# Sublayer boundaries, chunk sums and level differences put in another order in a two-layer hybrid decoder trunk

## What is computed

```python
for l in range(DEPTH):                       # DEPTH = 2
    mod = (silu(c) @ w_ada[l] + b_ada[l]).reshape(bsz, 3, 3, 1024)
    x = sublayer(x, ffn1)                    # swiglu: (silu(a) * b) @ w_out, width 2816
    x = sublayer(x, token_mixing)            # HGRN2, stick-breaking, dilated attention; gates; @ w_out
    x = sublayer(x, ffn2)
# sublayer: h = rms_norm(x, g_pre) * (1 + scale) + shift
#           x = x + res_w * gate * rms_norm(fn(h), g_post)
```

## Time and profile before

| what | value |
|---|---|
| median of 3 runs | 3118.58 us (3118.45 to 3123.26) |
| the profiled execution's own time | 3121.1 us |
| its span | 3119.3 us |
| PE busy | 2929.9 us (94%) |
| DVE busy | 1541.3 us (49%) |
| ACT busy | 1005.0 us (32%) |
| POOL busy | 193.1 us (6%) |
| SP's DMA queue | 32.4% of 16 engines |
| chain that ended last | PE 85%, DVE 7%, ACT 3%, issue 2% |
| granted TensorE clock, mean | 0.975 of full |

### The profile page before, as it was taken

How to read it: one execution, slowest core, us unless ns; L and a number is a source line. 1 busy time by engine, 2 the same in 40 slices (tenths; PEclk the granted TensorE clock), 3 DMA queues, 4 the chain that set the end, 5 groups by cost and what they waited for, 6 DMA issues and landing times.

```text
span 3119.3 us, 40607 instructions
## 1 busy us (share of the span) xinstructions
PE 2929.9 (94%) x16999; PEld 2558.1 (82%) x16999; DVE 1541.3 (49%) x2236; ACT 1005.0 (32%) x1455; POOL 193.1 (6%) x188
## 2 busy tenths in 40 slices
PE   6999898989999988999989989899899999899998
PEld 5888897777788788889988879877777887888897
DVE  5555236777344446542255552477753554453323
ACT  3322124444422323222242221354443232332212
...
GB/s 238 176 189 189 109 96 61 61 62 68 41 55 82 81 127 104 189 135 95 97 88 195 186 167 89 88 62 75 51 52 41 68 95 81 109 122 95 102 89 55
DMA packets 358854, 324.53 MB, mean 104 GB/s; under 512 B 12300, under 2 KB 305552, under 8 KB 357776
## 3 DMA queue, kind: packets, MB, share of 16 engines
q1 hardware_dynamic: 357136, 319.77, 32.4%
...
HBM read 313.43 MB, written 6.29 MB: 102 GB/s over the span
## 4 chain that ended last, share of the span: by engine, by line
PE 85%; DVE 7%; ACT 3%; issue 2%; POOL 0%; ACTq 0%; DVEq 0%; POOLq 0%
PE PS L769 25%; PE PS L771 24%; PE PS L770 24%; PE PS L973 2%; PE PS L786 2%; DVE WL L1573 1%; PE PS L1048 1%; PE PS L1010 1%; PE PS L1070 1%; PE PS L1034 1%; PE PS L1025 1%; PE PS L1022 1%; PE PS L832 1%; ACT WH L1164 1%; PE PS L779 1%
## 5 line engine op out<-in xcount | busy, mean ns | idle before, releaser
L769 PE MATMUL PS<-HH,WH 128*128 128x512 f32 (+1 forms) x2512 | 974.3, 388 | 27.3 <-DVE WL L1562 10.3
L771 PE MATMUL PS<-HH,WL 128*128 128x512 f32 (+1 forms) x2512 | 948.7, 378 | 0.0
L770 PE MATMUL PS<-HL,WH 128*128 128x512 f32 (+1 forms) x2512 | 946.9, 377 | 0.0
L1562 DVE TENSOR_TENSOR WL<-RAW,WH 128x2048 fp32r<-128x2048 f32 x142 | 325.5, 2292 | 515.5 <-ACT WH L1164 515.5
L769 PEld LDWEIGHTS PS<-HH,WH 128*128 128x128 f32 x2512 | 475.7, 189 | 116.7 <-DVE WL L1573 13.7
L771 PEld LDWEIGHTS PS<-HH,WL 128*128 128x128 f32 x2512 | 475.0, 189 | 88.7
L770 PEld LDWEIGHTS PS<-HL,WH 128*128 128x128 f32 x2512 | 476.1, 190 | 82.0 <-issue 2.9
L1164 ACT ACTIVATE WH<-RAW 128x2048 fp32r<-128x2048 f32 x142 | 271.8, 1914 | 792.6 <-PE PS L771 792.6
L769 PE MATMUL PS<-GH,WH 128*128 128x256 f32 x1408 | 405.0, 288 | 18.2 <-DVE WL L1562 17.5
L771 PE MATMUL PS<-GH,WL 128*128 128x256 f32 x1408 | 403.7, 287 | 0.0
L770 PE MATMUL PS<-GL,WH 128*128 128x256 f32 x1408 | 403.3, 286 | 0.0
...
## 6 DMA issues: line engine op xcount, KB each, us to landing
...
RAW<-in_w_in SPq DMA_DIRECT2D x132, 512.0 KB, 4.7
...
AWB<-in_w_ada SPq DMA_DIRECT2D x5, 2048.0 KB, 16.0
...
```

What stands on the lines that cost most here:

```text
L769: pe.matmul(o, ah, bh, start=start, stop=skip, skip_group_check=skip)
L770: pe.matmul(o, ah, bl, start=False, stop=skip, skip_group_check=skip)
L771: return pe.matmul(o, al, bh, start=False, stop=stop or skip, skip_group_check=skip)
L1562: dve.tensor_tensor(wl[:, 0:n], RAW[g % 2][:, 0:n], wh[:, 0:n].bitcast(F32), ALU.subtract).then_inc(w_low, 1)
```

## The change

- **Weight halves.** `from_stage` counts groups from the end e of a rows stage. Group e-2 is split into the second buffers (WXH, WXL) and e-1 into the slot of e-3's predecessor, both free once group e-4 is used; e goes to the slot of e-3, e+1 to the other second buffers.
- **Rows product.** The first row group goes by four columns at a time, (second half, j 4 to 7) first, each with its own wait for its banks; after `merge` these are waits for single products of br_mul.
- **Modulation.** In FFN 1 the last chunk's sum, its copy and its two column operations stand at mixing item 3, step 0, and the sums alternate banks 4 and 5.
- **Boundary.** A DVE addition halves each squared piece of x (`square_pair`, 128x256, 48 in all: 8 for each of five boundaries and 8 at the start), and `x_sum` is one matmul. The orders of squares, roots and pair additions on ACT and DVE move, and the second half's `x_sum` on PE goes one step earlier.
- **Mixing.** `a_diff` moves from POOL to DVE, one level ahead. The preparation stands behind the takes and its third step is cut in two (k = 3 and 4). Turning a tile moves from step 1 to 2 on PE and from 2 to 3 on DVE. Tiles 4 to 7 get banks of their own. The first branch group's low half stands in the last item at step 3.

The diff, without context, blank lines, the two hunks that only renumber `ada_cols`, and part of the indentation:

```diff
@@ -437,16 +437,15 @@
-def beside(g):
-    return g % NG in (G_MIX, G_MIX + 1, G_FFN2, G_FFN2 + 1) or (g % NG < 2 and now[0] + g // NG > 0)
+def from_stage(g):
+    g += NG * (now[0] > 0)
+    return min((g - e - n * NG for n in range(3) for e in ROW_ENDS if g - e - n * NG >= -2), default=99)
-    if beside(g):
-        back = max((e for e in ROW_ENDS if e <= g), default=0) - 3
-    else:
-        back = g - (4 if beside(g - 2) else 2)
+    d = from_stage(g)
+    back = g - {-1: 3, 0: 3, 1: 4, 2: 3, 3: 3}.get(d, 2)
@@ -456,7 +455,11 @@
-    return (WXH[g % 2], WXL[g % 2]) if beside(g) else (WH[g % 2], WL[g % 2])
+    d = from_stage(g)
+    if d in (-2, 1):
+        return WXH[d > 0], WXL[d > 0]
+    slot = (g + (d in (-1, 0))) % 2
+    return WH[slot], WL[slot]
@@ -475,7 +478,10 @@
-    return tile if tile < 4 else tile % 2
+    return tile if tile < 8 else tile % 2
+def ada_bank(f, i):
+    return 2 if (f, i) == (0, FI // 2 - 1) else 4 + i % 2
@@ -712,7 +718,8 @@
-            sp.wait_ge(ada_out, at(ada_out, ADA_CHUNKS[0]))
+            sp.wait_ge(ada_part, at(ada_part, KT * (ADA_CHUNKS[0] + 1)))
+            sp.wait_ge(ada_out, at(ada_out, ADA_CHUNKS[0] - 1))
@@ -781,10 +788,8 @@
-        pe.wait_ge(x_sq, at(x_sq, 8 * p + 4 * half + q + 1))
-        for e in range(2):
-            mm = pe.matmul(y_at(half, 0), ones, XSQ[q][:, e, :],
-                           start=(q == 0 and e == 0), stop=True, skip_group_check=True)
+        pe.wait_ge(x_pair, at(x_pair, 8 * p + 4 * half + q + 1))
+        mm = pe.matmul(y_at(half, 0), ones, XSQ[q][:, 0, :], start=(q == 0), stop=True, skip_group_check=True)
@@ -809,8 +814,10 @@
-                if not half and p and (u, i) == (1, 1) and k >= KT // 2:
-                    x_sum(p, 1, k - KT // 2)
+                if not half and p and (u, i) == (1, 1) and 3 <= k <= 5:
+                    x_sum(p, 1, k - 3)
+                    if k == 5:
+                        x_sum(p, 1, 3)
@@ -824,15 +831,6 @@
-        def ada(i):
-            pe.wait_ge(ada_part, at(ada_part, i * KT + (ADA_BEFORE[f] + 2) * KT))
-            pe.wait_ge(ada_out, at(ada_out, ADA_BEFORE[f] + i))
-            for q in range(4):
-                mm = pe.matmul(PS[:, 4, q:q + 1], AACC[i % 2][:, q * P:(q + 1) * P], ones[:, 0:1],
-                               start=True, stop=True)
-            mm.then_inc(ada_sum, 1)
@@ -840,16 +838,22 @@
-                    ada(i - 1)
-        if n == FI // 2:
-            ada(FI // 2 - 1)
-    def rows_product(g0, n, rh, rl, ready, b, bank_free=None):
+                    ada(f, i - 1)
+    def ada(f, i):
+        pe.wait_ge(ada_part, at(ada_part, i * KT + (ADA_BEFORE[f] + 2) * KT))
+        pe.wait_ge(ada_out, at(ada_out, max(ADA_BEFORE[f] + i - 1, 0)))
+        for q in range(4):
+            mm = pe.matmul(PS[:, ada_bank(f, i), q:q + 1], AACC[i % 2][:, q * P:(q + 1) * P], ones[:, 0:1],
+                           start=True, stop=True)
+        mm.then_inc(ada_sum, 1)
+    def rows_product(g0, n, rh, rl, ready, b, bank_free):
-            wh = WH[(g0 + i) % 2][:, :].rearrange("p (k c) -> p k c", k=2)
-            wl = WL[(g0 + i) % 2][:, :].rearrange("p (k c) -> p k c", k=2)
+            wh, wl = (w[:, :].rearrange("p (k c) -> p k c", k=2) for w in halves_of(g0 + i))
@@ -859,9 +863,9 @@
-            for half in (1, 0) if i == 0 else (0, 1):
-                for j in range(KT):
-                    if i == 0 and bank_free:
+            for half, j0 in ((1, 4), (0, 0), (0, 4), (1, 0)) if i == 0 else ((0, 0), (0, 4), (1, 0), (1, 4)):
+                for j in range(j0, j0 + 4):
+                    if i == 0 and j == j0:
@@ -899,8 +903,10 @@
+            if (half, j) == (1, 4):
+                pe.wait_ge(x_done, at(x_done, 8 * b))
-                pe.wait_ge(ada_out, at(ada_out, ADA_BEFORE[f] + chunks(l, f)))
+                pe.wait_ge(ada_out, at(ada_out, ADA_BEFORE[f] + chunks(l, f) - (chunks(l, f) == FI // 2)))
@@ -934,7 +940,7 @@
-        if k0 == 0:
+        if k0 == 0 and tile >= 8:
@@ -1084,7 +1090,7 @@
-        if k == 1 and m and TILE0[m] - 1 in TURN_OF:
+        if k == 2 and TILE0[m] - 1 in TURN_OF:
@@ -1127,9 +1133,10 @@
+    def merged_free(half, j):
+        pe.wait_ge(br_mul, at(br_mul, {(1, 4): KT - 2, (0, 0): KT - 1}.get((half, j), KT)))
-        if i == 0:
-            pe.wait_ge(br_mul, at(br_mul, KT))
@@ -1143,10 +1150,13 @@
+                if (m, k) == (3, 0):
+                    pe.wait_ge(*taken(2))
+                    ada(0, ADA_CHUNKS[0] - 1)
-        rows_product(G_WO, 4, lambda k: HH[:, k, :], lambda k: HL[:, k, :], merged, 3 * l + 1)
+        rows_product(G_WO, 4, lambda k: HH[:, k, :], lambda k: HL[:, k, :], merged, 3 * l + 1, merged_free)
@@ -1239,14 +1249,16 @@
-            if q in (1, 2) and not last:
-                square_x(b + 1, 0, 2 * q - 2)
-                square_x(b + 1, 0, 2 * q - 1)
-        root_y(b, 1)
+            if q < 2 and not last:
+                square_x(b + 1, 0, 2 * q)
+                square_x(b + 1, 0, 2 * q + 1)
+            root_y(b, 1)
+            if j == 1:
+                root_y(b, 1)
@@ -1497,6 +1509,11 @@
+    def square_pair(p, half, q):
+        dve.wait_ge(x_sq, at(x_sq, 8 * p + 4 * half + q + 1))
+        dve.tensor_tensor(XSQ[q][:, 0, :], XSQ[q][:, 0, :], XSQ[q][:, 1, :], ALU.add).then_inc(x_pair, 1)
@@ -1538,14 +1555,25 @@
-            if q:
-                pair_add(b, 1, q - 1)
+            if q and not last:
+                square_pair(b + 1, 0, q - 1)
+            if q in (1, 3):
+                pair_add(b, 1, q // 2)
+        if not last:
+            square_pair(b + 1, 0, 3)
+        pair_add(b, 1, 2)
-        inputs(b + 1, 0, lambda q: residual(b, 1, q))
+        def second(q):
+            residual(b, 1, q)
+            if q:
+                square_pair(b + 1, 1, q - 1)
+        inputs(b + 1, 0, second)
+        square_pair(b + 1, 1, 3)
@@ -1585,10 +1613,10 @@
+                if (i, u) == (FI // 2 - 1, 1) and n == FI // 2:
+                    ada_columns(f, i - 1)
-        for i in range(min(n, FI // 2 - 2), n):
-            ada_columns(f, i)
@@ -1617,7 +1645,7 @@
-        dve.tensor_copy(MOD[:, 4 * ch:4 * ch + 4], PS[:, 4, 0:4]).then_inc(ada_out, 1)
+        dve.tensor_copy(MOD[:, 4 * ch:4 * ch + 4], PS[:, ada_bank(f, i), 0:4]).then_inc(ada_out, 1)
@@ -1696,6 +1724,7 @@
+        if k == 4:
@@ -1713,6 +1742,16 @@
+    def a_diff(h, k):
+        n = A_LEVELS * h + k
+        dve.wait_ge(p_log, at(p_log, 3 * h + 3))
+        dve.wait_ge(v_decay, at(v_decay, max(n - 1, 0)))
+        w = P >> k
+        b = level_view(AB[h % 2][:, :], k)
+        dve.tensor_tensor(level_view(AD[n % 2][:, :], k), b,
+                           b[:, :, w // 2 - 1:w // 2].broadcast_to([P, SEQ // w, w]), ALU.subtract).then_inc(v_diff, 1)
@@ -1726,6 +1765,10 @@
+        if k == 0:
+            a_diff(h, 0)
+        if k + 1 < A_LEVELS:
+            a_diff(h, k + 1)
@@ -1869,14 +1912,14 @@
-        if (m, k) in PREPARE_AT:
-            a_prepare(*PREPARE_AT[(m, k)])
-        if k == 2 and m and TILE0[m] - 1 in TURN_OF:
+        if (m, k) in PREPARE_AT:
+            a_prepare(*PREPARE_AT[(m, k)])
+        if k == 3 and TILE0[m] - 1 in TURN_OF:
@@ -1907,6 +1950,9 @@
+        for q in range(4):
+            square_pair(0, half, q)
+    for half in range(2):
@@ -1915,18 +1961,24 @@
-        dve.wait_ge(ada_out, at(ada_out, ADA_CHUNKS[0]))
-        columns(l, 4 * ADA_FIRST, 4 * (ADA_ALL - ADA_OWN), 2, (1, 2), (0, 1))
-        dve.wait_ge(ada_cols, at(ada_cols, 7))
+        dve.wait_ge(ada_out, at(ada_out, ADA_CHUNKS[0] - 1))
+        columns(l, 4 * ADA_FIRST, 4 * (ADA_ALL - ADA_OWN - 1), 2, (1,), (0, 1))
+        dve.wait_ge(ada_cols, at(ada_cols, 6))
+                if (m, k) == (3, 0):
+                    ada_columns(0, ADA_CHUNKS[0] - 1)
+                    dve.wait_ge(ada_out, at(ada_out, ADA_CHUNKS[0]))
+                    columns(l, 4 * (ADA_ALL - ADA_OWN - 1), 4 * (ADA_ALL - ADA_OWN), 6, (2,), ())
+                    dve.wait_ge(ada_cols, at(ada_cols, 8))
+                if (m, k) == (NM - 1, 3):
+                    low(G_BR)
-        low(G_BR)
@@ -1958,25 +2010,12 @@
-    def a_diff(h, k):
-        n = A_LEVELS * h + k
-        pool.wait_ge(p_log, at(p_log, 3 * h + 3))
-        pool.wait_ge(v_decay, at(v_decay, max(n - 1, 0)))
-        w = P >> k
-        b = level_view(AB[h % 2][:, :], k)
-        pool.tensor_tensor(level_view(AD[n % 2][:, :], k), b,
-                           b[:, :, w // 2 - 1:w // 2].broadcast_to([P, SEQ // w, w]), ALU.subtract).then_inc(v_diff, 1)
-        if k < A_LEVELS:
-            a_diff(h, k)
```

More of the change, by code:

```diff
@@ L1948, in _ @@
                     dve.wait_ge(ada_out, at(ada_out, ADA_BEFORE[1] + chunks(l, 1)))
[L1949 to L1950 removed]
+                    columns(l, 4 * (ADA_ALL - ADA_OWN), 72, 8, (), (2,))
+                    dve.wait_ge(ada_cols, at(ada_cols, 10))
                     if l + 1 < DEPTH:
[L1952 to L1953 removed]
+                        columns(l + 1, 0, 4 * ADA_FIRST, 10, (0,), ())
```

(1 more changed line is left out.)

8 lines of the change are left out of this document (2 added, 6 removed).

## The result

| | before | changed |
|---|---|---|
| median | 3120.92 us (3118.45 to 3125.54) | 2991.52 us (2987.59 to 2996.35) |
| again, in a later run of both | 3120.02 us | 2988.49 us (2987.42 to 2989.18) |
| the profiled execution's own time | 3121.1 us | 2996.35 us |
| span | 3119.3 us | 2994.6 us |

The ratio is 0.9584, with a 95% interval of 0.9564 to 0.9605. The forecast was 2992 us.

What follows compares the result with a forecast made beforehand. PE, busy 94% of the span, bounds the kernel by its work, granted clock and idle time. Seven terms sum to 126.8 us, 3121.1 to 2994.3; the median stood 2.5 lower, so 2992 us was forecast, range 2974 to 3024.

Steps and rivals of the forecast that it cites:

- Joint phase: Ahead of six joint phases: 4.39 us waits for a group's low half go, 26.3 us, plus 13.2 of low clock: 39.5 us.
- Boundary: Pair sums to second half, five boundaries: 32.0 us for 39.3, less 0.4 for clock, 6.9 each: 34.5 us.
- the boundary stays a DVE chain: Rival: eight more additions between residuals and inputs, so each boundary gains 2 us, not 6.9: 3017 us; chance 0.10.
- The 0.4 us taken off for clock: In each boundary: average deduction for a low-clock stretch that may follow the new waits, 7.3 us gain becoming 6.9.
- Chunk sum: Modulation sum at the first FFN in: two waits, 15.2 us, go, with 1.8 of sums and 4.0 of clock: 21 us.
- Merge and into w_out: Merge: two waits shortened by 2.4 us each plus 5.4 of clock, 10.2; wait in front of w_out goes, 6.6 us.
- Mixing: Mixing heads: four heads gain 10 us, the other eight 5, less 2: 13 us, bounds -12 and +25.
- The 2 us taken off for bank and second turned cv item: In mixing: 1 us off in each layer for a tile's bank margin and DVE's softplus ahead of the second turned item.
- First inputs: At the start: eight square sums, 4.2 us, go, but eight DVE additions precede the first scaled input: 2 us, 0 to 4.
- The rival in which new waits pull it down: Rival: five boundaries and four heads each lose 2.5 us to one more low-clock stretch: 3014 us; chance 0.07.
- The shared port: DVE in mixing: POOL's differences stretch its instructions; moving them returns 40 us against 51 added, with QL's mean at 0.42.

Runs made afterwards that it cites:

- u_sums: The changed kernel with its new boundary orders, but two matmuls for each sum of squares and no halving additions on DVE: 3000.83 us.
- u_bound: The changed kernel with the old boundary: old orders on ACT, DVE and PE, two matmuls per sum of squares, no halving additions: 3035.86 us.
- i_order: The changed kernel with DVE scaling inputs 0 to 4 and forming low parts 0 to 3 ahead of the second half's first residual in five boundaries: 2976.03 us.
- u_chunk: The changed kernel with the last chunk's sum, its copy and two column operations back at the end of the first FFN in: 3016.14 us.
- u_merge: The changed kernel with the first branch group's low half back behind the last item and w_out's first row group waiting for the last branch product: 3003.58 us.
- a_again: The changed kernel itself, unaltered, measured again beside the others on the same chip to show its spread: 2988.49 us.
- u_pool: The changed kernel with the level differences back on POOL at their old place, all else kept: 3005.23 us.

## Why the prediction was right, and where its reasons were not

The forecast was 2992 us, the medians are 2991.52 and 2988.49, and term by term:

- **Joint phase, term 39.5:** as argued, wait and clock together; undoing it costs 38.9 by the trace and 44 in the medians.
- **Boundary, term 34.5:** measured 33.5. The waits of the order followed stood nearly as forecast: 0.2 at the first sum, 0.93 for YSQ, 2.0 for HL one column later, 1.9 at the third and fourth sums (1.47 measured), 0.6 at the fourth column (0.32), none ahead of the second half. But one reason failed: the text counted the eight matmuls saved in each boundary (0.52 us each, half of the 8.3) as work taken off PE's path. u_sums has them back and is no later at full clock. The gain is that of the orders, by u_bound, and i_order shows that DVE's chain is still the bound; that the moved orders gain by shortening this chain is argued, as they were undone all at once. The 0.4 us taken off for clock was 0.3: of the three low stretches in the first profile two cost nothing and one, behind PE's last wait (at 1539.8), 1.5 us. What the rival "the boundary stays a DVE chain" said of the mechanism was true; its price of 2 us was not.
- **Chunk sum, term 21:** 21.3 to 22.3 by the trace of u_chunk.
- **Merge and into w_out, terms 10.2 and 6.6:** 17.5 in the profiled execution of u_merge, 14 in the median. Merge's residual wait is 0.83, forecast 0.8.
- **Mixing, term 13:** 14.4 less 4.7 for merge's wait, plus 1.8 for the sums moved in, 11.5; by a_again's profile, whose mixings have less low clock, 17.6. The term lies between the two. Head 0 waits 2.21, 0.67 and 0.90 us for a forecast 2.5, 0.8 and 1.2. The 2 us taken off for bank and second turned cv item were wrong: PE has no wait there. That the term came out is in part luck: it named AS as the largest gain at hand, but AS and QL together fell by 0.8 us only, and the 5.2 us of VT, which it did not price, went whole. It also treated takes and differences as separate gains; each without the other keeps half of the waiting saved or less.
- **First inputs, term 2:** 1.7 between the two profiles, but undoing the halving at the start costs less than 1 us (u_sums reaches the first FFN out 262.1 us after the first sum, the changed kernel's two profiles 262.3 and 261.3). The clock differs there: the low level at the start ends at 65.3 us before, at 62.1 in u_sums, at 72.1 and 69.6 in the changed kernel. So what the halving alone is worth here stays open.
- **The clock:** 54.2 us of PE's work left the low level, 25 us at 0.46; the terms name 22.6 (13.2, 4.0 and 5.4) and hold part of the 4.7 behind AV. The rival in which new waits pull it down was partly there: three of five boundaries have a stretch of 3.4 us (at 1140.4, 1539.8 and 2604.7), the others none; a_again has one in four of five. The rival's price of 2.5 us each was too high: they cost 1.5 or nothing. The Trainium skill ("TensorE: Matmul & The Clock Gate", "HAM oscillation") tells of a kernel whose waits of some 3 to 5 us for a DMA between groups of matmuls lower the clock each time; in these traces a wait of 2.0 us with 0.93 before it does so in some boundaries and not in others.
- **The shared port.** QL's mean went to 0.415 us as forecast, and back to 0.641 with POOL's differences. The Trainium skill ("SBUF — State Buffer", "Who interferes with whom") says that VectorE instructions with two SBUF inputs and GpSimd instructions that read SBUF exclude each other; the traces agree: by that rule the 40 us came back, and 46 went again in u_pool.
